# Decoder step on one core: rotation per projection chunk, head transposes and prompt attention between projection rows, weight pieces and cache copies in another order

## What is computed

```python
q, k, v, z, gb = split_projection(h, w_in)      # one projection, 2048 x 6144
q, k = rope(q, pos), rope(k, pos)               # 8 heads x 128, halves of 64
att = combine_branches([branch(q, k, v, w // d, d) for w, d in ((128, 1), (512, 4), (2048, 16))])
conv = gb * short_conv(z_ext, conv_w, T)        # z = C * u, width 3
h = layer_norm(ALPHA * h + concat(att, conv) @ w_out)
h = layer_norm(ALPHA * h + peer_ffn(h, ...))    # expert rows gathered from two tables
return h + sigmoid(h @ w_gate) * (p @ w_ple), new_k, new_v, new_conv
```

## Time and profile before

| what | us |
|---|---|
| median of 3 runs | 2484.01 |
| lowest and highest | 2483.26 and 2498.29 |
| the profiled execution | 2487.67 |
| its span, first to last instruction | 2485.5 |
| PE, DVE, ACT, POOL busy | 1899.3, 1690.6, 976.7, 1114.0 |

### The profile page before, as it was taken

The page is one execution under the profiler, slowest core; times in us unless marked ns, Lnnn a source line. Parts: engine busy times, 40 slices in busy tenths (PEclk is TensorE's granted clock), DMA queues, the critical chain, the costliest instruction groups (busy, mean ns, idle before and its releaser), DMA issues.

```text
span 2485.5 us, 27261 instructions
## 1 busy us (share of the span) xinstructions
PE 1899.3 (76%) x10395; PEld 1571.3 (63%) x10395; DVE 1690.6 (68%) x2335; ACT 976.7 (39%) x1603; POOL 1114.0 (45%) x484
## 2 busy tenths in 40 slices
PE   6998899899969855345233331899999999999798
PEld 5875778787859735344133231777777777877676
DVE  1064222422146988887899999899988988997724
ACT  3223122223223221111299993644444444444332
POOL 3663233335636446787766887122221222211154
PEclk9998899899989987677655555999999999999899
DMA  9997999997999869899999999799999999998647
GB/s 343 390 382 265 377 415 416 374 393 263 362 361 354 322 262 409 353 421 422 421 379 384 420 421 372 269 386 375 384 371 347 343 365 365 402 371 302 210 186 262
DMA packets 131809, 883.58 MB, mean 355 GB/s; under 512 B 19011, under 2 KB 20611, under 8 KB 55589
## 3 DMA queue, kind: packets, MB, share of 16 engines
q1 hardware_dynamic: 76388, 479.23, 50.6%
q0 software_dynamic: 55296, 402.68, 40.3%
HBM read 871.28 MB, written 141.63 MB: 408 GB/s over the span
## 4 chain that ended last, share of the span: by engine, by line
issue 31%; PE 27%; DMA 14%; POOL 14%; DVE 13%; ACT 2%; POOLq 0%; SPq 0%; ACTq 0%; DVEq 0%
PE psum L1515 8%; PE psum L1517 8%; PE psum L1516 8%; DMA v_raw<-in_peer_v 7%; POOL w_lo L545 7%; POOL expert_rows L575 6%; DMA expert_rows<-in_peer_u,experts 6%; DVE expert_rows L1326 5%; DVE v_lo L1457 2%; DVE expert_rows L1392 2%; DVE x_tokens L1401 1%; PE psum L1856 1%; ACT v_hi L888 1%; DMA ansposed_expert_rows<-in_peer_u,experts 1%; DMA ple_tokens<-in_p_sample 1%
## 5 line engine op out<-in xcount | busy, mean ns | idle before, releaser
L545 POOL TENSOR_TENSOR w_lo<-w_raw,w_hi 128x2048 fp32r<-128x2048 f32 x80 | 374.4, 4680 | 465.7 <-ACT w_hi L606 465.7
L575 POOL DMA_INDIRECT expert_rows<-in_peer_u,experts x238 | 469.1, 1971 | 184.7 <-DVE expert_rows L1326 114.6
L1515 PE MATMUL psum<-v_hi,gate_matrix_hi 128*128 128x512 f32 x1024 | 406.4, 397 | 36.5 <-DVE v_lo L1457 36.2
L888 ACT ACTIVATE v_hi<-v_raw 128x1024 fp32r<-128x1024 f32 x256 | 271.4, 1061 | 404.2 <-DMA v_raw<-in_peer_v 320.5
L1326 DVE SCALAR_TENSOR_TENSOR expert_rows<-expert_rows,x_tokens 128x2048 f32<-128x2048 f32 x174 | 393.4, 2289 | 45.8 <-DMA expert_rows<-in_peer_u,experts 43.6
L1516 PE MATMUL psum<-v_lo,gate_matrix_hi 128*128 128x512 f32 x1024 | 400.0, 391 | 0.0
L1517 PE MATMUL psum<-v_hi,gate_matrix_lo 128*128 128x512 f32 x1024 | 399.9, 390 | 0.0
L1457 DVE TENSOR_TENSOR v_lo<-v_raw,v_hi 128x1024 fp32r<-128x1024 f32 x256 | 310.4, 1221 | 81.1 <-ACT v_hi L888 80.2
L606 ACT ACTIVATE w_hi<-w_raw 128x2048 fp32r<-128x2048 f32 x80 | 153.2, 1915 | 382.8 <-PE psum L1517 309.1
L1515 PEld LDWEIGHTS psum<-v_hi,gate_matrix_hi 128*128 128x128 f32 x1024 | 192.8, 188 | 101.2 <-issue 39.9
L1811 PE MATMUL psum<-one_hot_first_gated,one_hot_second 128*128 128x128 f32 x448 | 107.8, 417 | 170.2 <-ACT one_hot_first_gated L792 167.0
(11 more groups left out here) (336 smaller groups left out, 3512.8 us busy)
## 6 DMA issues: line engine op xcount, KB each, us to landing
v_raw<-in_peer_v SPq DMA_DIRECT2D x256, 512.0 KB, 7.1
out<-in_state_attn_k SPq DMA_DIRECT2D x64, 1020.0 KB, 10.1
out<-in_state_attn_v SPq DMA_DIRECT2D x64, 1020.0 KB, 10.9
w_raw<-in_w_in SPq DMA_DIRECT2D x48, 1024.0 KB, 8.1
cache_part<-in_k_parts SPq DMA_DIRECT2D x40, 1024.0 KB, 10.2
cache_part<-in_v_parts SPq DMA_DIRECT2D x40, 1024.0 KB, 12.5
w_raw<-in_w_out SPq DMA_DIRECT2D x16, 1024.0 KB, 6.7
w_raw<-in_peer_wq SPq DMA_DIRECT2D x16, 1024.0 KB, 7.1
```

The costliest lines, as they stand in the source:

```text
L545: nc.gpsimd.tensor_tensor(l_, r_, h_.bitcast(f32), ALU.subtract).then_inc(w_lo_ready, 1)
L575: pool.indirect_dma_start(ring[slot_of(n)][:, :], None, u_tab, bass.IndirectOffsetOnAxis(idx_p[:, t - 1, j:j + 1], 0)).then_inc(u_in[slot_ ...
L888: A(vhi[m % HS][:, :], vrl[m % RL][:, :], ACT.Copy).then_inc(vh_ok, 1)
L1515: MM(out, lh, rh, start=start, stop=False)
```

## The change

- VectorE rotates chunk by chunk: all three tiles of 512 columns after each of chunks 0 to 3, in 18 small instructions.
- The 16 groups of head transposes go between the 16 rows of chunk 5, through banks 3 and 7. For that the decode tokens of the input projection have a place of their own (`dec0`).
- Pieces 24 to 27 are cut into rows, and the 16 rows stand between the steps of the prompt attention, whose value products move to banks 2 and 3. ScalarE splits pieces 26 to 29 between the heads.
- Pieces 28 and 29 stand ahead of batch 0; batches 0 to 5 have no third piece, 6 and 7 have. SP loads three more pieces ahead of the batches instead of one, and in all one less by their end, so piece 50 is loaded behind them.
- VectorE does the next batch's maximum ahead of a batch's output, and the chunk copies one batch earlier.
- SP writes the new keys before, the new values after the head transposes. Of the 14 copies ahead of the prompt attention 6 stay and 2 come later in it; four batches instead of eight have a copy; two more stand in the last wq chunk, five ahead of the third v piece, three in the gate projection.

```diff
-GAP = (1, 0, 1, 1, 0, 1, 1, 1)
+GAP = (0, 0, 0, 0, 0, 0, 1, 1)
...
+QK_BANKS = (3, 7)
...
+    dec0 = at("decode_in_T", [128, KT, 2 * TS], f32r, 72 * KB)
     dec = at("decode_T", [128, KT, 2 * TS], f32r, 108 * KB)
...
             sp.dma_start(okp, qkv_p[:, :, DA:2 * DA]).then_inc(out_s, 16)
+            for b in range(NB):
+                sp.dma_start(oks[b, PAST - NS:PAST, :], qkv_s[b * NS:(b + 1) * NS, DA:2 * DA]).then_inc(out_s, 16)
+            copies(6)
+            sp.wait_ge(out_s, 16 * (1 + NB))
+            sp.wait_ge(qk_T, 16)
+            load_part(0)
+            load_w(26)
+            sp.wait_ge(acc_free, 6)
             sp.dma_start(ovp, qkv_p[:, :, 2 * DA:3 * DA]).then_inc(out_s, 16)
             for b in range(NB):
-                sp.dma_start(oks[b, PAST - NS:PAST, :], qkv_s[b * NS:(b + 1) * NS, DA:2 * DA]).then_inc(out_s, 16)
                 sp.dma_start(ovs[b, PAST - NS:PAST, :], qkv_s[b * NS:(b + 1) * NS, 2 * DA:3 * DA]).then_inc(out_s, 16)
-            load_w(26)
             load_w(27)
-            copies(14)
-            sp.wait_ge(out_s, 16 * (2 + 2 * NB))
-            sp.wait_ge(qk_T, 16)
-            load_part(0)
+            copies(2)
             sp.wait_ge(s_score, HEADS)
             load_part(1)
             load_part(2)
+            load_w(28)
+            load_w(29)
+            sp.wait_ge(out_s, 16 * (2 + 2 * NB))
             sp.wait_ge(s_po, HEADS)
             for n in range(3, KVS):
                 load_part(n)
-            part, piece = [KVS], [28]
+            part, piece = [KVS], [30]
...
-            next_piece()
+            for _ in range(3):
+                next_piece()
             for b in range(NB):
                 next_parts()
                 next_piece()
                 next_piece()
                 next_parts()
-                if GAP[b]:
+                if GAP[b] and b + 1 < NB:
                     next_piece()
-                copies(1)
+                copies(b % 2)
...
-                load_chunk(wq, c, 64 + c * PPC, 2 if c == 0 else 0, (2, 1, 2, 1))
+                load_chunk(wq, c, 64 + c * PPC, 2 if c == 0 else 0, (2, 2, 2, 2) if c == 3 else (2, 1, 2, 1))
...
+                    sp.wait_ge(u_free, len(VEC_ROWS))
+                    copies(5)
...
-                load_chunk(w_gate, c, 80 + c * PPC, 2 if c == 0 else 0, (2, 2, 1, 1) if c == 0 else (1, 1, 0, 0), W_GATE)
+                load_chunk(w_gate, c, 80 + c * PPC, 2 if c == 0 else 0, (2, 2, 1, 1) if c == 0 else (1, 1, 1, 0), W_GATE)
...
-            his(2, 24)
-
-            for j in range(16):
+            A(thi[:, :, 0:TS], dec0[:, :, 0:TS].bitcast(f32), ACT.Copy)
+            A(tlo[:, :, 0:TS], dec0[:, :, TS:2 * TS].bitcast(f32), ACT.Copy).then_inc(dec_T, 1)
+            his(2, 20)
+            def head_copies(j):
+                bank = QK_BANKS[j % 2]
                 act.wait_ge(qk_T, j + 1)
-                A((qs, ks)[j % 2][:, j // 2, :], PS[:, 2 + j % 6, 0:TS], ACT.Copy)
-                A((qp, kp)[j % 2][:, j // 2, :], PS[:, 2 + j % 6, TS:N], ACT.Copy).then_inc(qk_ok, 1)
+                A((qs, ks)[j % 2][:, j // 2, :], PS[:, bank, 0:TS], ACT.Copy)
+                A((qp, kp)[j % 2][:, j // 2, :], PS[:, bank, TS:N], ACT.Copy).then_inc(qk_ok, 1)
+            for k in range(PPC):
+                for j in range(4 * k, 4 * k + 4):
+                    head_copies(j)
+                hi(22 + k, k % 2)
...
+                if e == 1:
+                    hi(26 + h // 2, (h // 2) % 2)
             def exps(b):
                 act.wait_ge(d_neg, b + 1)
@@ -669,7 +688,7 @@
                     m = A(osb[32 * i:32 * i + 16, :], PS[32 * i:32 * i + 16, 3, 0:256], ACT.Copy)
                 m.then_inc(d_out, 1)
-            nxt = [26]
+            nxt = [30]
...
+            def rope(c):
+                hd = 4
+                cc = slice(c * CW, (c + 1) * CW)
+                dve.wait_ge(acc_free, c + 1)
+                halves, products = [], []
+                for t in range(3):
+                    r = TILES[t][1]
+                    src = (qkv_s[:, cc] if t == 0 else qkv_p[:, t - 1, cc]).rearrange("p (h d) -> p h d", h=hd)
+                    x1, x2 = src[:, :, 0:DH // 2], src[:, :, DH // 2:DH]
+                    cb = cosb[0:r, t, :].unsqueeze(1).broadcast_to([r, hd, DH // 2])
+                    sb_ = sinb[0:r, t, :].unsqueeze(1).broadcast_to([r, hd, DH // 2])
+                    tm = [rtmp[0:r, j, 256 * t:256 * (t + 1)].rearrange("p (h d) -> p h d", h=hd) for j in range(4)]
+                    for j, (a, b) in enumerate(((x1, cb), (x2, sb_), (x2, cb), (x1, sb_))):
+                        m = V.tensor_tensor(tm[j], a, b, ALU.mult)
+                    halves.append((x1, x2))
+                    products.append(tm)
                 link(m)
-                V.tensor_tensor(x1, tm[0], tm[1], ALU.subtract)
-                link(V.tensor_tensor(x2, tm[2], tm[3], ALU.add))
+                for (x1, x2), tm in zip(halves, products):
+                    V.tensor_tensor(x1, tm[0], tm[1], ALU.subtract)
+                    m = V.tensor_tensor(x2, tm[2], tm[3], ALU.add)
+                link(m)
             for c in range(4):
                 token_copies(c)
-            dve.wait_ge(acc_free, 4)
-            dve.wait_ge(c2_in, 160)
-            rope(1)
-            rope(2)
+                if c == 0:
+                    dve.wait_ge(c2_in, 160)
+                rope(c)
+            V.memset(nmx[:, :, :], 0.0).then_inc(rope_ok, 1)
...
+            u_copies(6)
             prompt_out(HEADS - 1)
...
-            u_copies(6)
+            u_copies(7)
+            masked_max(1)
             decode_out(0)
-            masked_max(1)
             normalise(1)
             masked_max(2)
             decode_out(1)
-            u_copies(7)
             normalise(2)
+            conv_inputs(8)
+            masked_max(3)
             decode_out(2)
-            masked_max(3)
             normalise(3)
-            conv_inputs(8)
+            masked_max(4)
             decode_out(3)
-            masked_max(4)
             normalise(4)
+            conv_inputs(9)
             masked_max(5)
             decode_out(4)
-            conv_inputs(9)
             normalise(5)
             convolution()
+            masked_max(6)
             decode_out(5)
-            masked_max(6)
             normalise(6)
             conv_gates(10)
...
+                    if kk == KP - 1 and 2 in tiles:
+                        m.then_inc(w_used, 1)
+                    if between is not None:
+                        between(q)
...
+            def head_transposes(j):
+                if j == 0:
+                    pe.wait_ge(rope_ok, 1)
+                if j >= 2:
+                    pe.wait_ge(qk_ok, j - 1)
                 col = (j % 2) * DA + (j // 2) * DH
                 for t in range(3):
                     c0, r = TILES[t]
                     src = qkv_s[:, col:col + DH] if t == 0 else qkv_p[:, t - 1, col:col + DH]
-                    m = TR(PS[:, 2 + j % 6, c0:c0 + r], src, ident[0:r, 0:r])
+                    m = TR(PS[:, QK_BANKS[j % 2], c0:c0 + r], src, ident[0:r, 0:r])
                 m.then_inc(qk_T, 1)
+            for h in range(2):
+                for k in range(PPC):
+                    in_piece(h * 4 + k, k, 4 * h)
+            chunks(in_piece, 2, 1, True)
+            pe.wait_ge(acc_free, 3)
+            for k in range(PPC):
+                in_piece(16 + k, k, 0)
+            pe.wait_ge(acc_free, 4)
+            for k in range(PPC):
+                in_piece(20 + k, k, 4, head_transposes)
             pe.wait_ge(qk_ok, 16)
...
+            rows = [0]
+            def next_rows(count):
+                for _ in range(count):
+                    k, kk = divmod(rows[0], KP)
+                    feature_rows(24 + k, k, 4, kk)
+                    rows[0] += 1
+            pe.wait_ge(acc_free, 5)
             prompt_scores(0)
             prompt_scores(1)
+            pe.wait_ge(dec_T, 1)
+            pe.wait_ge(acc_free, 6)
+            next_rows(1)
             pe.wait_ge(s_neg, 1)
             prompt_scores(2)
+            next_rows(1)
             for h in range(HEADS):
                 e = h % 2
                 if h + 3 < HEADS:
                     pe.wait_ge(s_neg, h + 2)
                     prompt_scores(h + 3)
                 pe.wait_ge(s_prob, h + 1)
+                if h >= 2:
+                    pe.wait_ge(s_po, h - 1)
                 for a in range(3):
                     m = TR(PS[:, 2 + e, a * 128:(a + 1) * 128], psm[:, e, a, :], ident[:, :])
                 m.then_inc(s_pT, 1)
+                if h + 1 < HEADS:
+                    next_rows(1)
                 pe.wait_ge(s_pok, h + 1)
-                if h >= 2:
-                    pe.wait_ge(s_po, h - 1)
                 vals = lambda t: qkv_p[:, t, 2 * DA + h * DH:2 * DA + (h + 1) * DH]
-                MM(PS[:, 4 + e, 0:128], vals(0), ppt[:, e, 0, :], start=True, stop=True)
```

(13 more changed lines are left out.)

56 lines of the change are left out of this document (18 added, 38 removed).

## The result

The changed kernel takes 2503.99 us (median of 16 executions) beside 2486.05 for the kernel before on the same chip: ratio 1.0066, 95% interval 1.0049 to 1.0083. It is slower by 16 to 18 us, where 20.6 less were predicted: within 1%, but on the other side and outside the predicted range. The profiled execution took 2512.61 us (span 2510.8), 8.6 more than its median.

The account below looks back on a forecast made before the run. Bounds seen: a softmax chain in the prompt attention; TensorE and the transfer queue almost together in the batches. Terms -24.3 + 2.7 + 1 = -20.6 from the median 2484.0 gave 2463.4, say 2463 us; range 2446 to 2478.

Parts of the forecast that it names:

- Step 4: Decode batches: the queue becomes the bound, batch 1's to batch 7's scores 213 to 197.4 us; output projection 24.3 us earlier.
- The term before it, batch 0: First decode batch, without a third piece: 27.1 us on TensorE, its keys all loaded by then.
- rival D: Batches: TensorE waits for keys at six boundaries, clock low for half of each batch; 46 us more, 2509; chance 0.05.
- step 2: Head transposes between chunk 5's rows: 16 groups at 0.47 us, 7.5 us on the path, projection ends at 217.5.
- step 3: Prompt attention with feature rows between its steps: 48 us plus 7 of stalls (POOL lock, late piece 26), bounds 0 and 20.
- Step 1: Rotation per chunk on VectorE in the input projection: cost 0, bounds -2 to +3 us; head transposes find it done.
- Step 5: Output projection: weight piece 50, now queued behind the token tiles, lands later; +2.7 us, bounds 0 and 6.
- Step 6: Ten copies moved to later places: +1 us in the last query chunk, bounds 0 and 5; 0 elsewhere.
- C: After the batches: the time is given back, ten copies at 2.6 us each, 26 us, leaving 2489; chance 0.07.
- A: Covers hold better: no prompt attention stall, queue at 2.55 us a unit, no later losses; 2448; chance 0.22.
- B: Prompt attention stretched by POOL's blocks and late piece 26, softmax the bound again: 20 us, 2476; chance 0.20.

Follow-up runs that it names:

- spread_only: Kernel before, its eight batch copies moved to the third v piece (five ahead) and the gate chunks (three): ratio 1.0003 to the kernel before.
- rows_between_keys: Changed kernel with two of the first feature piece's four rows ahead of the waits for the fourth and fifth key part, batches 1 to 6: ratio 0.9990.
- early_pieces: Changed kernel with rows between keys, tail moves undone, batch copies in the prompt attention; then two copies later, pieces 28 and 30 issued earlier: ratio 0.9869.
- tail_undone: Changed kernel with piece 50 again ahead of the token tiles and two copies moved from the last query chunk to the third v piece: ratio 1.0010.
- warm: Changed kernel with matmuls that compute nothing ahead of the waits for the fourth and fifth key part in batches 1 to 6: ratio 1.0030.

## Why the prediction was wrong

**Step 4 failed**, in "the queue becomes the bound": scores(1) to scores(7) was put at 76 units of 2.60 us, 197.4, and took 213.4. That is 16.0 of the 28.3 us by which the output projection's start was missed (579.2 for 550.9). Two premises fell. The first was that a share of 0.98 means a stretch bound by bytes: spread_only took 6 of 82 units out and nothing moved. The second was that TensorE has slack at a boundary (27.1 of work against 32.9 of queue). The keys do not come when the queue has time, they come when slots are free. No term of the sum stood for the wait for a slot. The arithmetic of what happened instead is in the windows: three pieces fewer are 21 us less of work, but TensorE's busy time fell only from 198.8 to 188.7, since it ran at 0.91 and not 0.97 (rows_between_keys, at 0.97, needs 178.9), and its waits grew from 14.2 to 24.7. The three pieces had stood where TensorE waits anyway. Step 4 also counts five boundaries without a third piece; there are six whose waits lie between S1 and S7, as rival D has it.

The term before it, batch 0, was put at 27.1 and took 31.4, because piece 30 was late (16.6 us of waiting on ScalarE, 2.70 on TensorE): 4.3 more; early_pieces, with piece 30 there in time, shows the 27.1. The two pieces ahead of it took 15.8 for 14.1, at a clock of 0.87; that is chance in part, since tail_undone and warm, with the same code there, take 14.2. Behind S7, 41.3 for 39.8; spread_only, unchanged there, has 41.3 too. With the 1.9 of step 2 and the 2.8 of step 3 these make up the 28.3, but for rounding.

**Step 3** was put at 55 us and took 57.8 (219.4 to 277.2), 56.2 to 56.8 in the profiles of kernels that are alike there. Both mechanisms were there, the lock (VectorE's 128x2 instruction at 222.73 took 3.63 us and ended with POOL's, at 226.36) and piece 26 late by 4.6; 7 for stalls was too little by 1 to 3. The Trainium skill, SBUF — State Buffer, section "SBUF: two separate sides", has the second user of the shared ports wait until the first one's instruction ends; the trace agrees to 0.01 us.

**Step 2** had the mechanism right and the price low: 16 groups took 9.4 us (210.0 to 219.4), 0.59 each for 0.47.

**Step 1** was right: head transposes found the rotation done, and no wait for it is left.

**Step 5** was put at +2.7, and measured +6: at its upper bound. Its sum has a slip, since 3.65 MB at 2.5 us per MB are 9.1 us and not 11. The transfer took longer still: ScalarE split piece 50 at 593.91, 14.8 us behind the start of the output projection, where it was 10.3 before. **Step 6**, the last query chunk, was put at +1, bounds 0 and 5, and measured +7. Its reasoning looked at the share of the transfer engines during the chunk (0.79); but the transfers land in the order in which SP issues them (all of them from 395 to 500 us in the profile after), and what follows the copies is a transfer for which TensorE already waited 8.3 us. Copies ahead of a known wait lengthen it. The five copies ahead of the third v piece cost nothing, as predicted (ScalarE does not wait for that piece), nor do the three in the gate chunks (163.6 us from the last v piece to the end, 163.1 before), and the room of the first place is now known: five fit, seven do not (2.3 us of wait).

**The rivals.** D had the right place and sign, but far too high a price: the clock does fall at every boundary, for some 6 us and not for half a batch. Warm puts 6.4 us of S1 to S7 on it, the busy times of rows_between_keys 9.8. The prediction argued that a slower TensorE gives the queue time and removes the next wait. It doesn't: the slow matmuls stand ahead of the batch's value products, which then come later, and with them the slots. No run parts this step from the rest. The Trainium skill, TensorE: Matmul & The Clock Gate, section "HAM oscillation — how this bites in real kernels", advises, for a loop whose tiles begin cold after a wait for their transfer, to do more of the work between two waits so that TensorE stays warm; no run here tries that. The trace agrees on the cold start: the granted clock is 0.50 from 432 to 436 us, behind waits of 0.53 and 2.88. What was tried, giving TensorE work inside the waits, was worth 19 us. C, the time given back later, was true in part: two of the ten copies cost 7 us, the other eight nothing. A and B did not come up: what they disputed was small beside step 4. (On the chances: the prediction puts a third of its own forecast below 2459 and then counts two fifths; a third gives 0.37 for faster, not 0.41.)

## What to carry to other kernels

A busy share near 1 on the transfer engines does not show that bytes bound a stretch: ask what each transfer waits for before it is issued, and whether what it waits for is freed early or late in the loop. Work that a change takes out of a loop is only won if it did not stand in front of a wait; look at what comes next on that engine and when it will be there. Put the work that is left where the wait is (here rows of a projection between the keys), and put no copies in front of a transfer that something already waits for.

## What was not expected of the hardware

Two short waits of TensorE within one stretch of scores, such as 0.53 and 2.88 us, went with some 6 us at 1.2 GHz in each batch (431 to 438 in batch 4); with throwaway matmuls in them the granted clock was 1.00 for 207 us. A small instruction of VectorE, on 128x2 elements, is held by POOL as long as a large one: 3.63 us, where it takes 0.17 in the other heads. And the expert stage took 742.0 to 755.4 us from the first to the last v_hi in the profiles of kernels that are the same there (five copies ahead of the third v piece), so a difference of 10 us in it between two profiles says nothing of an edit.
